# Two moves in TensorE's order and one in the load order of a hybrid decoder step: keys turned later, merge gates cut by contraction tile, one weight block ahead of a cached block

## The chip, the cores and the metric

The kernel runs on one core of one Trainium2 chip. The metric is device time in microseconds (us): the median of three runs. One more execution was taken by the hardware profiler; its span goes from its first instruction to its last.

## What is computed

One inference step of a two-layer decoder, on 256 prompt tokens and 8 sequences of 8 new tokens each (320 columns in all). Each layer runs two token mixers side by side, merges them by gates, and then a gated ConvFFN:

```
hq, hf, hi, hg, nq, kc, vc, ks, vs, kw, vw, ngate, mgate = jnp.split(h @ w_in, splits, axis=-1)
o_hg, s_hg = hgrn2_mixer(...)                     # state recurrence over chunks, one state per head
q = rope_partial(heads(nq, NSA_HEADS), pos)
new_slc = jnp.stack([rope_partial(heads(ks, NSA_KV_HEADS), pos), heads(vs, NSA_KV_HEADS)], axis=2)
kw = rope_partial(heads(kw, NSA_KV_HEADS), pos)
o_win = window_sample(q, pos, kw, vw, past[2])    # samples: window cache and the new rows
o_cmp, o_slc = nsa_cmp_slc(q, pos, cmp_rows, slc_rows, cmp_pe, cmp_w1, cmp_w2)
branches = jnp.einsum('blnc,ncd->blnd', jnp.stack([o_hg, o_nsa], axis=2), w_branch)
mg = jax.nn.sigmoid(mgate.astype(jnp.float32)).reshape(B, L, N_BRANCH, D_MODEL).astype(h.dtype)
merged = jnp.sum(mg * branches, axis=2)
return merged @ w_out, (new_cmp, new_slc, new_win, s_hg)
```

The two parts that matter here are the rotation of queries and keys (`rope_partial`) ahead of the attention scores, and the merge gates (`mgate`): 16 feature tiles per layer, each 128 columns of `w_in` against all 1024 input features.

## The kernel before

Everything is laid out with features on the partitions and the 320 tokens along the free dimension. Each engine has its program written out by hand, layer by layer (`layer(l)` in each block), and the engines meet through semaphores. **TensorE** goes through the layer in this order: input projections, the levels of the HGRN2 recurrence (`level`), the compressor rows (`compressed_rows`), the attention of the prompt in four units (`scores`, `turned`, `values`), the attention of the samples in two halves of four sequences (loop `hb`, from L1179), the HGRN2 outputs, the branch and output projections, the FFN.

PSUM is two rings of four banks, `mm` and `ax`. `mm_plan` and `ax_plan` (L126) list every tile in the order in which it is filled, and name the engine that empties it (V is VectorE, A is ScalarE). A tile may begin when the tile four places ahead of it in its ring has been emptied; `begin` waits for that. ScalarE and VectorE empty tiles in their own programs, in the order of these plans.

Weights and cached rows pass through a ring of four SBUF slots in the order of `BLOCKS` (L67); block n goes to slot n mod 4. SyncE walks `BLOCKS` in its `layer`: at block n it waits until that block's last reader is done (`LAST_USE`), then issues the load of block n + 4 into the slot. So the place of a block in the list sets what its successor's load waits for. `mgN` holds the merge-gate columns of feature tiles 2N and 2N + 1, `kv0` and `kv1` the cached rows of the two halves, `st0` and `st1` the old HGRN2 states of the samples for heads 0, 1 and heads 2, 3 (1 MB each), `br0` and `br1` the branch projection. `LAST_USE` of `mgN` is the gate tile `mgb{2N+1}`, of `kv0` and `kv1` the value products `ov5` and `ov7`.

**Keys.** GpSimd rotates the keys in `stok` in three pieces (L2312 to L2318) and counts `k_roped` (L2319). TensorE transposes them as `kt0` and `kt1` (L1091): six transposes that wait for the third `k_roped`. They stand between `compressed_rows(0)` and `compressed_rows(1)`. Behind `compressed_rows(1)` come the four products `nqr0` to `nqr3`, which permute the queries for their rotation; then `rows_turned(NSEQ)` (tile `cp`), `compressed_rows(2)`, and the compressor's hidden layer. ScalarE empties `kt0` (L1419), VectorE `kt1` (L1939) ahead of `nqr0` to `nqr3`.

**Merge gates in the sample stage.** A gate tile is eight products, one per 128 input features (`feature_tile`). Gates 4 to 7 are made later from split operands. Of gates 0 to 3 the sample stage makes six tiles, three in each half, where other engines are busy with the softmax:

```
GATES = [[(1, 0), (1, 1), (2, 0)], [(2, 1), (3, 0), (3, 1)]]
```

In half `hb` with n = 4 + 2 hb the order is: keys of the cached rows transposed (`skt`), state products (`ds`), `sample_scores(n)`, gate, `sample_scores(n+1)`, `sample_turned(n)`, gate, `sample_values(n)`, `sample_turned(n+1)`, gate, `sample_values(n+1)`. In the first half four of the first gate's eight products stand ahead of `turned(3)` instead. In the second half `sample_rows_turned(1)` (tile `ovt1`) follows, then `prompt_outputs` and `sample_outputs`, which reads `st0` and, from its head 2 on, `st1`.

The helper at L671 records all matmuls, the one at L674 all transposes, so in the rows below those two lines stand for many places.

Of the kernel before, what the change touches and what calls it, by code (L numbers as in the profile page):

```python
# [37 lines left out]
ACT = mybir.ActivationFunctionType  # L38
AX = mybir.AxisListType

P = 128
# [4 lines left out]
KD = D // P  # L46
# [17 lines left out]
DOWN = [[6, 6, 6, 4], [6, 8, 8]]  # L64


BLOCKS = (["par", "w_hf", "w_hq", "w_nq", "cmp", "w_hi", "w_kvn", "w_kvc", "w_cmp", "w_hg", "kv0", "mg0", "mg1", "kv1",  # L67
           "st0", "mg2", "st1", "br0", "mg3", "br1", "wo0", "wo1"] + [f"ff{n}" for n in range(NJ // JPB)]
          + [f"dn{mh}_{n}" for mh in range(2) for n in range(len(DOWN[mh]))])
NBLK = len(BLOCKS)  # L70
# [56 lines left out]
def ax_plan():  # L127
    out = [("cst", "V"), ("norm1", "A"), ("rst", "V")]
    out += level_plan(0) + level_plan(1) + level_plan(2) + [(f"cc{s}", "A") for s in range(4)]
    out += level_plan(3) + level_plan(4) + level_plan(5) + level_plan(6) + [(f"cc{s}", "A") for s in range(4, NSEQ)]  # L130
    out += [("kt0", "A"), ("kt1", "V")] + [(f"nqr{m}", "V") for m in range(4)]
    out += [("cp", "A"), ("hidk", "A"), ("hidv", "A"), ("gsel0", "V"), ("gsel1", "V")]
    out += [("kcm", "A")] + [(f"vc{n}", "A") for n in range(3)] + [("kcr", "V")]
    out += [(f"krt{h}", "AV"[h % 2]) for h in range(HH)] + [("scc0", "V"), ("scc1", "V")]

    def turned(n):
        return [(f"tp{n}_{x}", "AV"[x % 2]) for x in range(2 * (UNITS[n][0] + 1))] + [(f"tpc{n}", "A")]

    def scored(n):
        return [(f"sc{n}_{e}", "V") for e in range(4)]  # L140

    out += scored(0) + scored(1) + turned(0) + scored(2) + [("ov0", "V")] + turned(1) + [("ov1", "V")] + turned(2)
    out += scored(3) + [("ov2", "V")]
    for hb in range(2):
        out += [(f"skt{hb}_{x}", "A" if hb == 0 else "AV"[x % 2]) for x in range(4)] + ([("ovt0", "V")] if hb else [])
        out += turned(3) if hb == 0 else []
        out += [(f"ds{c}", "V") for c in (2 * hb, 2 * hb + 1)] + ([("ov3", "V")] if hb == 0 else [])
        n = 4 + 2 * hb
        out += [(f"ss{x}{n + g}", "A") for g in range(KVH) for x in "ab"]
        out += [(f"tps{n}", "V"), (f"tpn{n}", "A"), (f"ov{n}", "V"), (f"tps{n + 1}", "V"), (f"tpn{n + 1}", "A"),  # L150
                (f"ov{n + 1}", "V")] + ([("ovt1", "V")] if hb else [])
    out += [("op0", "V"), ("op1", "V"), ("os0", "V"), ("os1", "V")]
    for h in range(HH):
        if h == 2:
            out += [(f"xt{x}", "V") for x in range(HH)]
        out += [(f"dsa{h}", "V"), (f"dsb{h}", "V")]
    for n in range(2):
        out += [(f"br{x}{m}", "V") for x in "ba" for m in range(4 * n, 4 * n + 4)]
    out += [("norm2", "A")]
    out += [(f"cv{n}", "V") for n in range(6)]  # L160
    return out + [(f"dn1_{m}", "V") for m in range(4)]
# [73 lines left out]
def hybrid_step(nc, x_prompt, x_sample, cache_cmp, cache_slc, cache_win, state_hgrn, state_conv, page_table, norm_mix,  # L235
# [4 lines left out]
    with ctx:  # L240
# [420 lines left out]
        def _(pe):  # L661
# [50 lines left out]
                              k == KD - 1)  # L712
                last.then_inc(mm_full[L], 1)

            def feature_tile(name, w, cols, half=None):

                bank = MM[L].bank(name) if half == 1 else begin(MM[L], name)
                for k in range(KD) if half is None else range(4 * half, 4 * half + 4):
                    last = mm(bank[:, 0:T], cols(w, k), hT[:, k, :], k == 0, k == KD - 1)
                if half != 0:  # L720
                    last.then_inc(mm_full[L], 1)

            def end_sums(tiles):
# [186 lines left out]
                        last = tr(bank[:, P * x:P * x + P], oX[x][:, h, :])  # L910
                    last.then_inc(ax_full[L], 1)

            def merge_gate(m, y, l, half=None):
                mg = f"mg{m // 2}"
                if m % 2 == 0 and y == 0:
                    pe.wait_ge(*landed_at(mg, l))
                w = kt_of(mg, KD, 512)
                feature_tile(f"mg{'ab'[y]}{m}", w, plain(w, 256 * y + P * (m % 2)), half)

            def level(kk):  # L920
                m = LEVELS[kk]
# [134 lines left out]
            def layer(l):  # L1056
# [31 lines left out]
                for q in range(4, NSEQ):  # L1088
                    rows_turned(q)
                compressed_rows(0, l)  # L1090
                for x in range(2):  # L1091
                    bank = begin(AXR[L], f"kt{x}")
                    if x == 0:
                        pe.wait_ge(k_roped[L], 3)
                    for i in range(3):
                        last = tr(bank[:, P * i:P * i + TM[i]], stok[0:TM[i], i, 256 * x:256 * x + P])
                    last.then_inc(ax_full[L], 1)
                compressed_rows(1, l)
                for m in range(4):
                    bank = begin(AXR[L], f"nqr{m}")  # L1100
                    pe.wait_ge(*MM[L].emptied_at(f"nq{m}"))
                    mm(bank[:, 0:T], con("perm"), qraw[:, m, :], True, True).then_inc(ax_full[L], 1)
                rows_turned(NSEQ)
                compressed_rows(2, l)

# [73 lines left out]
                for hb in range(2):  # L1179
# [6 lines left out]
                            last = tr(bank[:, P * y:P * y + P], kv[:, w, 2 * bp + y // 2, y % 2, 0:P])  # L1186
                        last.then_inc(ax_full[L], 1)
                    if hb == 0:
                        merge_gate(*GATES[0][0], l, 0)
                        turned(3)  # L1190
                    else:
                        sample_rows_turned(0)
# [13 lines left out]
                    pe.wait_ge(*AXR[L].emptied_at(f"skt{hb}_2"))  # L1206
                    n = 4 + 2 * hb
                    sample_scores(n, hb, 0)
                    merge_gate(*GATES[hb][0], l, None if hb else 1)
                    sample_scores(n + 1, hb, 1)  # L1210
                    sample_turned(n)
                    merge_gate(*GATES[hb][1], l)
                    sample_values(n, hb, 0)
                    sample_turned(n + 1)
                    merge_gate(*GATES[hb][2], l)
                    sample_values(n + 1, hb, 1)
                    if hb:
                        sample_rows_turned(1)

                pe.wait_ge(s_ready[L], 3)  # L1220
# [92 lines left out]
        def _(sc):  # L1313
# [38 lines left out]
            def layer(l):  # L1352
# [56 lines left out]
                for i in range(3):  # L1409
# [4 lines left out]
                    else:  # L1414
                        A(gts[0:SMP, i, :], bank[SMP:P, 116:140], ACT.Sigmoid)
                        A(ctok[0:SMP, i, 140:256], bank[SMP:P, 0:116], ACT.Copy)
                        A(ctok[0:SMP, i, 0:140], bank[0:SMP, 0:140], ACT.Copy).then_inc(*st.up(mm_act[L]))
                    if i == 0:
                        bank = take(AXR[L], "kt0")  # L1419
                        A(ktn[:, 0, :], bank[:, 0:T], ACT.Copy).then_inc(*st.up(ax_act[L]))  # L1420
                    if i == 1:
                        sc.wait_ge(*st.settled())
                        pair_rows(NSEQ, ctok[:, 0:2, :])
                        bank = take(AXR[L], "cp")
                        A(cmp_rows(NSEQ), cmp_bank(bank), ACT.Copy).then_inc(*st.up(ax_act[L]))

# [223 lines left out]
        def _(ve):  # L1650
# [63 lines left out]
            def layer(l):  # L1714
# [221 lines left out]

                link(V.tensor_tensor(qL[:, :, :], qH[:, :, :], pH[:, :, :], ALU.mult))
                ve.sem_inc(*st.up(ql_ready[L]))
                bank = take(AXR[L], "kt1")  # L1939
                V.tensor_copy(ktn[:, 1, :], bank[:, 0:T]).then_inc(*st.up(ax_dve[L]))  # L1940
                for m in range(4):
                    bank = take(AXR[L], f"nqr{m}")
                    V.tensor_tensor(qT[:, m, :], bank[:, 0:T], con("sinq"), ALU.mult).then_inc(*st.up(ax_dve[L]))
                for m in range(4):
                    link(V.tensor_tensor(qraw[:, m, :], qraw[:, m, :], con("cosq"), ALU.mult))
                    V.tensor_tensor(qT[:, m, :], qT[:, m, :], qraw[:, m, :], ALU.add).then_inc(*st.up(q_ready[L]))
# [532 lines left out]
```

## Time and profile before

| | |
|---|---|
| three runs | 1179.44, 1179.52, 1180.67 us; median 1179.52 us |
| profiled execution | 1179.78 us, of which the span is 1178.0 us |
| TensorE (PE) busy | 1148.1 us, 97% of the span; mean granted clock 0.99 |
| TensorE weight loads (PEld) | 1036.2 us, 88% |
| VectorE (DVE) / ScalarE (ACT) / GpSimd (POOL) | 706.7 us, 60% / 544.7 us, 46% / 174.1 us, 15% |
| chain of work that ended last | PE 91% |
| HBM traffic | 143 GB/s over the span |

TensorE is busy almost throughout, so a microsecond is won or lost where it waits, or where its granted clock is below full. The lists below come from one execution: a start and a length in us, the engine, the line, output<-input; the bracket at a row's end is the engine's idle time before it and who ended it. Rows of the second layer lie some 571 us behind those of the first.

### The profile page before, as it was taken

Reading aid. Unit: us, or ns where it says so; the run is one execution under the profiler, and the core shown is the slowest. Engines: PE = TensorE matmul, PEld = TensorE weight load, DVE = VectorE, ACT = ScalarE, POOL = GpSimd, SP = SyncE. Lnnn points to the kernel's source line nnn. Section 1 sums busy time; section 2 is a strip of 40 time slices with the busy share of each in tenths; the row PEclk is TensorE's granted clock in tenths of the full one; section 3 lists DMA queues with packets and bytes.
Section 4 is the critical chain, followed back from the end, with each engine's and each line's share of the span. In section 5 each row is a group of like instructions: output and inputs, shape, how many; then the busy total and the mean of one; then the engine's idle time right before and its main releaser. Section 6 shows DMA issues by size and latency. Waiting matters only on the chain.

```text
span 1178.0 us, 21121 instructions
## 1 busy us (share of the span) xinstructions
PE 1148.1 (97%) x8613; PEld 1036.2 (88%) x8613; DVE 706.7 (60%) x1302; ACT 544.7 (46%) x867; POOL 174.1 (15%) x300
## 2 busy tenths in 40 slices
PE   6999999999999999999999999999999999999997
PEld 5987767678999999999999777667899999999997
DVE  5686255457567777763568633644756677777442
ACT  4532256464355555533454223664634555555232
POOL 1154300002120100100114441000311110010000
PEclk9999999999999999999999989999999999999998
DMA  9554422157644444334456525203784445432411
GB/s 289 163 148 164 155 73 72 42 167 209 237 143 144 143 144 145 124 127 158 144 126 208 170 73 177 72 1 110 198 275 148 143 157 160 158 131 90 145 59 45
DMA packets 151498, 165.99 MB, mean 141 GB/s; under 512 B 31492, under 2 KB 114214, under 8 KB 151078
## 3 DMA queue, kind: packets, MB, share of 16 engines
q1 hardware_dynamic: 151402, 164.64, 44.7%
q8 instruction: 68, 1.11, 0.4%
q14 instruction: 28, 0.23, 0.1%
HBM read 156.22 MB, written 12.46 MB: 143 GB/s over the span
## 4 chain that ended last, share of the span: by engine, by line
PE 91%; DVE 3%; POOL 1%; DMA 1%; ACT 1%; issue 1%; SPq 0%; DVEq 0%; POOLq 0%; ACTq 0%
PE mm L671 65%; PE ax L671 23%; PE ax L674 4%; DMA ring<-in_state_conv 1%; ACT mixb L1317 1%; DMA ring<-in_state_hgrn 1%; POOL rtmp L2315 0%; DVE ring_low L1674 0%; POOL rtmp L2312 0%; POOL work L2318 0%; DVE mixb L1824 0%; DVE mixb L2089 0%; ACT attb L1317 0%; POOL work L2317 0%; DVE work_parts L2058 0%
## 5 line engine op out<-in xcount | busy, mean ns | idle before, releaser
L671 PE MATMUL mm<-work_parts 128*128 128x320 f32 (+2 forms) x1120 | 356.4, 318 | 1.1 <-DVE h_low L1668 1.1
L1674 DVE TENSOR_TENSOR ring_low<-ring,work_parts 128x2048 fp32r<-128x2048 f32 (+2 forms) x116 | 256.0, 2207 | 125.4 <-ACT work_parts L1317 124.7
L671 PE MATMUL mm<-h_low,work_parts 128*128 128x320 f32 x1024 | 319.2, 312 | 0.0
L671 PE MATMUL mm<-work_parts,ring_low 128*128 128x320 f32 x1024 | 315.5, 308 | 0.0
L1317 ACT ACTIVATE work_parts<-ring 128x2048 fp32r<-128x2048 f32 (+2 forms) x116 | 211.9, 1826 | 159.6 <-PE mm L671 90.3
L671 PEld LDWEIGHTS mm<-work_parts 128*128 128x128 f32 (+1 forms) x1120 | 209.1, 187 | 9.2 <-issue 2.0
L671 PEld LDWEIGHTS mm<-h_low,work_parts 128*128 128x128 f32 x1024 | 192.9, 188 | 0.3
L671 PEld LDWEIGHTS mm<-work_parts,ring_low 128*128 128x128 f32 x1024 | 193.0, 188 | 0.0
L671 PE MATMUL ax<-act_parts,work_parts 128*128 128x320 f32 x544 | 126.1, 310 | 0.6 <-DVE ring L2080 0.6
L671 PE MATMUL mm<-act_parts,work_parts 128*128 128x320 f32 x480 | 117.4, 310 | 0.3 <-DVE merged_low L2058 0.3
L671 PE MATMUL mm<-hT,ring 128*128 128x320 f32 x384 | 111.9, 445 | 0.0
L671 PEld LDWEIGHTS mm<-hT,ring 128*128 128x128 f32 x384 | 72.6, 194 | 29.8 <-issue 3.4
L671 PEld LDWEIGHTS ax<-act_parts,work_parts 128*128 128x128 f32 x544 | 92.0, 188 | 2.5 <-DVE ring_low L1674 2.2
L671 PE MATMUL mm<-act_parts,ring_low 128*128 128x320 f32 x304 | 93.9, 309 | 0.0
L671 PE MATMUL ax<-act_parts,ring_low 128*128 128x320 f32 x304 | 93.9, 309 | 0.0
L1317 ACT ACTIVATE attb<-attb,prm 128x256 f32<-128x256 f32 x88 | 41.1, 514 | 92.4 <-DVE attb L2178 92.4
L671 PEld LDWEIGHTS mm<-act_parts,work_parts 128*128 128x128 f32 x480 | 82.9, 188 | 0.8 <-DVE merged_low L2058 0.8
L1317 ACT ACTIVATE attb<-ax 128x512 f32<-128x512 f32 (+4 forms) x56 | 34.4, 675 | 49.9 <-PE ax L674 44.0
L671 PEld LDWEIGHTS mm<-act_parts,ring_low 128*128 128x128 f32 x304 | 57.1, 188 | 0.0
L671 PEld LDWEIGHTS ax<-act_parts,ring_low 128*128 128x128 f32 x304 | 57.1, 188 | 0.0
L2345 POOL TENSOR_TENSOR ring<-ring,mixb 128x1024 f32<-128x1024 f32 x8 | 15.2, 1917 | 244.3 <-PE ax L671 244.3
L2184 DVE TENSOR_TENSOR attb<-mm,work 128x320 f32<-128x320 f32 x44 | 21.7, 492 | 49.3 <-PE mm L671 49.3
(235 smaller groups left out, 1593.6 us busy)
## 6 DMA issues: line engine op xcount, KB each, us to landing
ring<-in_w_gate_up SPq DMA_DIRECT2D x44, 1024.0 KB, 6.9
ring<-in_w_in SPq DMA_DIRECT2D x10, 2048.0 KB, 8.3
ring<-in_w_in SPq DMA_DIRECT2D x18, 1024.0 KB, 7.7
ring<-in_w_down SPq DMA_DIRECT2D x8, 1536.0 KB, 6.7
ring<-in_w_out SPq DMA_DIRECT2D x4, 2048.0 KB, 13.8
ring<-in_w_down SPq DMA_DIRECT2D x4, 2048.0 KB, 8.6
ring<-in_w_in SPq DMA_DIRECT2D x32, 128.0 KB, 3.1
ring<-in_cache_cmp_kv SPq DMA_DIRECT2D x32, 128.0 KB
```

The costliest lines, as they stand in the source:

```text
L671: return nc.tensor.matmul(out, lhsT, rhs, start=start, stop=stop)
L674: return nc.tensor.transpose(out, in_, ident[0:in_.shape[0], 0:in_.shape[0]])
L1317: return nc.scalar.activation(out, in_, f, **kw)
L1674: V.tensor_tensor(unit_of(u, ring_r), unit_of(u, ring), unit_high(u).bitcast(F32), ALU.subtract).then_inc(*st.up(w_low[l]))
L2184: V.tensor_tensor(ut, bank[:, 0:T], rs[:, 0:T], ALU.mult).then_inc(*st.up(mm_dve[L]))
L2345: G.tensor_tensor(s0, s0, end.to_broadcast([P, NSEQ, HD]), ALU.mult).then_inc(*st.up(decayed[L]))
```

## The change

Three edits. `merge_gate` takes a range of products instead of a half.

- `kt0` and `kt1` move behind `nqr0` to `nqr3` in TensorE's order, in `ax_plan` and in the orders of ScalarE and VectorE.
- The 24 gate products of each half are cut at other points (`merge_products`): 3, 7, 7, 7 in the first half, 8, 7, 7, 2 in the second, where the last two stand behind `sample_values(7)`. Before they stood 4, 4, 8, 8 and 8, 8, 8.
- `mg0` and `kv0` change places in `BLOCKS`.

```diff
-"w_hg", "kv0", "mg0", "mg1", "kv1",
+"w_hg", "mg0", "kv0", "mg1", "kv1",
...
-    out += [("kt0", "A"), ("kt1", "V")] + [(f"nqr{m}", "V") for m in range(4)]
+    out += [(f"nqr{m}", "V") for m in range(4)] + [("kt0", "A"), ("kt1", "V")]
...
-            def feature_tile(name, w, cols, half=None):
+            def feature_tile(name, w, cols, first=0, end=KD):
-                bank = MM[L].bank(name) if half == 1 else begin(MM[L], name)
-                for k in range(KD) if half is None else range(4 * half, 4 * half + 4):
+                bank = MM[L].bank(name) if first else begin(MM[L], name)
+                for k in range(first, end):
                     last = mm(bank[:, 0:T], cols(w, k), hT[:, k, :], k == 0, k == KD - 1)
-                if half != 0:
+                if end == KD:
                     last.then_inc(mm_full[L], 1)
...
+            def merge_products(hb, at, n, l):
+
+                for g in range(3):
+                    first, end = max(at - KD * g, 0), min(at + n - KD * g, KD)
+                    if first < end:
+                        merge_gate(*GATES[hb][g], l, first, end)
...
                     if hb == 0:
-                        merge_gate(*GATES[0][0], l, 0)
+                        merge_products(0, 0, 3, l)
                         turned(3)
...
                     sample_scores(n, hb, 0)
-                    merge_gate(*GATES[hb][0], l, None if hb else 1)
+                    merge_products(hb, 0 if hb else 3, 8 if hb else 7, l)
                     sample_scores(n + 1, hb, 1)
                     sample_turned(n)
-                    merge_gate(*GATES[hb][1], l)
+                    merge_products(hb, 8 if hb else 10, 7, l)
                     sample_values(n, hb, 0)
                     sample_turned(n + 1)
-                    merge_gate(*GATES[hb][2], l)
+                    merge_products(hb, 15 if hb else 17, 7, l)
                     sample_values(n + 1, hb, 1)
                     if hb:
+                        merge_products(1, 22, 2, l)
                         sample_rows_turned(1)
```

On TensorE, first layer, behind the end of `compressed_rows(0)` (its products with 256 and 24 columns): the rows with `k_roped_0` are `kt0` and `kt1`, the four with 320 columns `nqr0` to `nqr3`. Before:

```order
L671 MATMUL mm<-ring,hT 128x24 x8
L674 MATMUL ax<-consts,work 128x128 [waits k_roped_0,ax_emptied_by_act_0]
...
L671 MATMUL mm<-ring,hT 128x256 [waits mm_emptied_by_act_0]
L671 MATMUL mm<-ring,hT 128x256 x7
L671 MATMUL mm<-ring,hT 128x24 x8
L671 MATMUL ax<-work,consts 128x320 [waits mm_emptied_by_dve_0,ax_emptied_by_act_0] x3
```

Now:

```order
L671 MATMUL mm<-ring,hT 128x256 [waits mm_emptied_by_act_0]
L671 MATMUL mm<-ring,hT 128x256 x7
L671 MATMUL mm<-ring,hT 128x24 x8
L671 MATMUL ax<-work,consts 128x320 [waits mm_emptied_by_dve_0,ax_emptied_by_act_0] x4
L674 MATMUL ax<-consts,work 128x128 [waits k_roped_0,ax_emptied_by_dve_0]
L674 MATMUL ax<-consts,work 128x128
```

The wait for the keys stands behind 16 + 4 products that stood behind it. In the second layer the rows are the same.

On TensorE, at the end of the second half's gates, up to `ovt1` (the transpose out of `attb`) and `prompt_outputs` (out of `mixb`); the first row belongs to `sample_turned(7)`, the 320-column rows are gate products, the rest between them is `sample_values(7)`:

```order
 L674 MATMUL ax<-consts,pcs 15x128
+L671 MATMUL mm<-hT,ring 128x320
 L671 MATMUL mm<-hT,ring 128x320 [waits mm_emptied_by_act_0]
-L671 MATMUL mm<-hT,ring 128x320 x7
+L671 MATMUL mm<-hT,ring 128x320 x5
 L671 MATMUL ax<-work,attb 128x64 [waits ax_emptied_by_act_0,ax_emptied_by_dve_0]
 L671 MATMUL ax<-work,attb 128x64
 L671 MATMUL ax<-work,attb 32x64 x4
 L671 MATMUL ax<-ring,work 32x64 x16
+L671 MATMUL mm<-hT,ring 128x320 x2
 L674 MATMUL ax<-consts,attb 128x128 [waits ax_emptied_by_dve_0]
```

The last product of the last gate, `mgb3`, stands behind `sample_values(7)` now; it stood ahead of it.

On SyncE, first layer, behind the loads of `kv1`: the state rows are `st0`, then `st1`; the `w_in` rows are `mg2`; `w_branch` (`br0`), not shown, follows:

```order
 L481 DMA ring<-in_cache_win_kv 128x512
-L481 DMA ring<-in_state_hgrn 128x8x128 [waits ax_full_0]
+L481 DMA ring<-in_state_hgrn 128x8x128 [waits mm_full_0]
 L481 DMA ring<-in_state_hgrn 128x8x128
-L481 DMA ring<-in_w_in 128x8x256 [waits mm_full_0]
+L481 DMA ring<-in_w_in 128x8x256 [waits ax_full_0]
 L481 DMA ring<-in_w_in 128x8x256
 L481 DMA ring<-in_state_hgrn 128x8x128 [waits mm_full_0]
```

`st0` waits for a gate now (`mgb1`), and `mg2` for `ov5`. `st1` waits for `mgb3` in both versions.

## Rows read from the trace of the kernel before

**Rows 1.** The page: busy us, share of the span, instructions.

```profile
PE 1148.1 (97%) x8613; PEld 1036.2 (88%) x8613; DVE 706.7 (60%) x1302; ACT 544.7 (46%) x867; POOL 174.1 (15%) x300
```

**Rows 2.** Waits of TensorE: us in total, times, longest.

```profile
PE ax L674 <- POOLq L2319: 5.7, 2, 2.8
PE ax L674 <- DVE attb L2034: 2.7, 2, 1.4
...
PE ax L674 <- DVE attb L2044: 0.9, 2, 0.4
...
PE ax L671 <- DMA ring<-in_state_hgrn: 0.6, 1, 0.6
```

**Rows 3.** Timeline, first layer: `compressed_rows(0)`, keys, `compressed_rows(1)`.

```profile
114.18 5.32 PE L671 MATMUL mm<-ring,hT 128*128 128x256 f32 x32
122.34 1.31 PE L674 MATMUL ax<-consts,work 128*128 128x128 f32 x6 [2.85 <-POOLq L2319]
123.59 6.88 PE L671 MATMUL mm<-ring,hT 128*128 128x256 f32 x32
```

**Rows 4.** Timeline, second layer: the keys.

```profile
693.97 1.87 PE L674 MATMUL ax<-consts,work 128*128 128x128 f32 x6 [2.84 <-POOLq L2319]
```

**Rows 5.** Windows: us, busy time of each engine, PEclk, DMA share, GB/s.

```profile
119.50:135.03 15.53, 12.69 (x82) 10.57 (x84) 4.18 (x10) 3.11 (x7) 4.81 (x10) 0.89 0.24 69
...
215.09:223.40 8.31, 8.31 (x67) 5.91 (x68) 3.58 (x18) 5.65 (x16) 0.00 (x0) 0.79 0.00 1
786.20:792.84 6.64, 6.64 (x68) 4.83 (x68) 3.58 (x18) 5.65 (x16) 0.00 (x0) 1.00 0.00 0
```

**Rows 6.** Window of the second layer behind the wait for the keys.

```profile
694.00:700.00 6.00, 6.00 (x16) 4.30 (x17) 0.49 (x1) 0.44 (x1) 2.83 (x1) 0.50 0.37 112
```

**Rows 7.** Timeline, sample stage: first half's first gate piece and wait; second half; one whole gate.

```profile
209.55 2.42 PE L671 MATMUL mm<-hT,ring 128*128 128x320 f32 x8
...
214.68 0.35 DVE L2034 TENSOR_SCALAR attb<-attb,wt 128x256 f32<-128x256 f32 x1
...
215.09 1.36 PE L674 MATMUL ax<-consts,attb 128*128 128x128 f32 x6 [1.35 <-DVE attb L2034]
...
240.77 0.35 DVE L2034 TENSOR_SCALAR attb<-attb,wt 128x256 f32<-128x256 f32 x1
...
241.71 0.87 PE L674 MATMUL ax<-consts,attb 128*128 128x128 f32 x6
...
793.66 4.47 PE L671 MATMUL mm<-hT,ring 128*128 128x320 f32 x16
```

**Rows 8.** Timeline, second layer, `sample_values(7)` to `sample_outputs`; SPq is SyncE's queue.

```profile
823.01 0.90 PE L671 MATMUL ax<-work,attb 64*128 64x64 f32 x12
823.11 0.99 SPq L481 DMA_DIRECT2D ring<-in_state_hgrn  x2
824.56 2.28 SPq L481 DMA_DIRECT2D ring<-in_w_branch  x3
824.93 0.30 PE L674 MATMUL ax<-consts,attb 128*128 128x128 f32 x1 [0.44 <-DVE attb L2044]
828.96 0.65 PE L671 MATMUL ax<-ring,mixb 128*32 128x128 f32 x16
830.23 0.64 PE L671 MATMUL ax<-ring,mixb 128*32 128x128 f32 x16 [0.63 <-DMA ring<-in_state_hgrn]
```

**Rows 9.** Timeline, first layer: loads of `st0` and `st1`, and the head of `sample_outputs`.

```profile
230.17 1.02 SPq L481 DMA_DIRECT2D ring<-in_state_hgrn  x2
...
253.67 0.99 SPq L481 DMA_DIRECT2D ring<-in_state_hgrn  x2
...
259.52 1.08 PE L671 MATMUL ax<-ring,mixb 128*32 128x128 f32 x32
```

**Rows 10.** DMA issues of `st0`, first layer: both, then the first alone; KB, median us to landing.

```profile
ring<-in_state_hgrn SPq DMA_DIRECT2D x2, 512.0 KB, 4.7
...
ring<-in_state_hgrn SPq DMA_DIRECT2D x1, 512.0 KB, 4.0
```

More of the change, by code:

```diff
@@ L64 @@
 DOWN = [[6, 6, 6, 4], [6, 8, 8]]
-BLOCKS = (["par", "w_hf", "w_hq", "w_nq", "cmp", "w_hi", "w_kvn", "w_kvc", "w_cmp", "w_hg", "kv0", "mg0", "mg1", "kv1",
+BLOCKS = (["par", "w_hf", "w_hq", "w_nq", "cmp", "w_hi", "w_kvn", "w_kvc", "w_cmp", "w_hg", "mg0", "kv0", "mg1", "kv1",
            "st0", "mg2", "st1", "br0", "mg3", "br1", "wo0", "wo1"] + [f"ff{n}" for n in range(NJ // JPB)]
@@ L911, in outputs_turned, with merge_gate @@
                     last.then_inc(ax_full[L], 1)
-            def merge_gate(m, y, l, half=None):
+            def merge_gate(m, y, l, first=0, end=KD):
                 mg = f"mg{m // 2}"
-                if m % 2 == 0 and y == 0:
+                if m % 2 == 0 and y == 0 and first == 0:
                     pe.wait_ge(*landed_at(mg, l))
                 w = kt_of(mg, KD, 512)
-                feature_tile(f"mg{'ab'[y]}{m}", w, plain(w, 256 * y + P * (m % 2)), half)
+                feature_tile(f"mg{'ab'[y]}{m}", w, plain(w, 256 * y + P * (m % 2)), first, end)
+            def merge_products(hb, at, n, l):
[3 more added lines that the diff above has]
+                        merge_gate(*GATES[hb][g], l, first, end)
             def level(kk):
@@ L1090, in layer @@
                 compressed_rows(0, l)
+                compressed_rows(1, l)
+                for m in range(4):
+                    bank = begin(AXR[L], f"nqr{m}")
+                    pe.wait_ge(*MM[L].emptied_at(f"nq{m}"))
+                    mm(bank[:, 0:T], con("perm"), qraw[:, m, :], True, True).then_inc(ax_full[L], 1)
                 for x in range(2):
@@ L1097, in layer @@
                     last.then_inc(ax_full[L], 1)
[L1098 to L1102, printed above, removed]
                 rows_turned(NSEQ)
@@ L1423, in layer @@
                         pair_rows(NSEQ, ctok[:, 0:2, :])
+                        bank = take(AXR[L], "kt0")
+                        A(ktn[:, 0, :], bank[:, 0:T], ACT.Copy).then_inc(*st.up(ax_act[L]))
                         bank = take(AXR[L], "cp")
@@ L1943, in layer @@
                     V.tensor_tensor(qT[:, m, :], bank[:, 0:T], con("sinq"), ALU.mult).then_inc(*st.up(ax_dve[L]))
+                bank = take(AXR[L], "kt1")
+                V.tensor_copy(ktn[:, 1, :], bank[:, 0:T]).then_inc(*st.up(ax_dve[L]))
                 for m in range(4):
```

5 lines of the change are left out of this document (removed).

## The prediction

> **What bounds the kernel now.** Read the page first: TensorE is busy 1148.1 of 1178.0 us [rows 1]. The busy sum of the matmuls does not tell where the time could come from, so the second view is the list of TensorE's own waits. One stands out, and it comes once per layer: transposes that wait for GpSimd's line 2319, 5.7 us in two. That line is the count of rotated keys, so these are `kt0`. Next come 2.7 us in two for VectorE's line 2034, the scaled probabilities of the samples, and 0.9 us in two for line 2044 [rows 2]. The third view is the timeline around each wait, and the fourth the granted clock there, since a wait can cost more than its length. In the first layer `compressed_rows(0)` takes 5.32 us; its twin `compressed_rows(1)`, the same products, takes 6.88 us right behind the wait [rows 3]. The windows say why: from 119.5 to 135.03 the mean granted clock is 0.89, and in the second layer six us behind the wait run at 0.50, the 1.2 GHz level [rows 5, 6]. So the price of a wait is its idle time and, sometimes, some microseconds at half clock behind it.
>
> The sum is made against the profiled execution, 1179.8 us (span 1178.0 and 1.8 around it), which lies 0.3 us above the median of the runs. A change below 0.2%, 2.4 us, would pass for no change; faster means below 1177.1, slower above 1181.9.
>
> **Keys behind the queries.** TensorE ends `compressed_rows(0)` at 114.18 + 5.32 = 119.5 and could transpose keys only at 122.34 [rows 3]. Now `compressed_rows(1)` comes first: 5.32 us at full clock, to 124.8, 2.5 us behind the keys, with `nqr0` to `nqr3` still to come. In the second layer the wait begins at 693.97 - 2.84 = 691.13 [rows 4]; 5.32 us more is 696.4, again 2.5 us behind. Both waits go: 2.85 + 2.84 = 5.7 us. With them goes the half clock: 0.11 of the 15.53 us in the first layer is 1.7 us, and half of the 6.0 us in the second is 3.0 us [rows 5, 6]. The moved instructions are the same six transposes, one ScalarE and one VectorE copy per layer, at no new cost. What is new is that `kt0` waits for VectorE to have emptied `nqr0`, which it does while TensorE still makes `nqr2` and `nqr3`, and that ScalarE copies `kt0` between the new compressor rows and `cp`; TensorE has `compressed_rows(2)` to do meanwhile. I take nothing for that; if the cover failed, the bounds are nothing and the length of the wait it replaces. **Gain 10.4 us.**
>
> **Gate pieces, first half.** The wait for line 2034 stands at `sample_turned(4)`. The scores end at 209.55, the scaled probabilities at 214.68 + 0.35 = 215.03, a chain of 5.5 us on VectorE and ScalarE. TensorE had four gate products and the next scores to do, until 215.09 - 1.35 = 213.74 [rows 7]. Now it has seven products. One product is 4.47 / 8 = 0.56 us [rows 7], three are 1.7 us, more than the 1.35 us, with 0.3 us to spare. Both waits go, 2.7 us. Behind it the first layer's clock fell and the second's did not: the same work takes 8.31 us at 0.79 and 6.64 us at 1.00 [rows 5], so 1.7 us more go. **Gain 4.4 us.** The pieces elsewhere get one product thinner. In the second half the piece ahead of `sample_turned(6)` keeps its eight, and there the margin is 241.71 - 241.12 = 0.6 us [rows 7]. No other wait shows in these places; between nothing and 0.56 us in each I take 0.2 us in all.
>
> **Two products ahead of `ovt1`.** The transpose at 824.93 waited 0.44 us for line 2044, in both layers [rows 2, 8]. Two products, 1.1 us, now cover that. **Gain 0.9 us.**
>
> **`st1` comes later.** This is the step that costs. `st1` goes into the slot of `mg1`, and SyncE loads it when `mgb3` is done. In the second layer that was at 823.01; the load went out at 823.11, and TensorE needed head 2 at 828.96 + 0.65 = 829.6 and got it at 830.23, so it paid 0.63 us [rows 8]. The budget was 6.6 us, the landing took 7.1 us from the first issue. Now the last two products of `mgb3` stand behind `sample_values(7)`. What lay between them and `ovt1`, 823.01 to 824.93, is lost from the budget: 6.6 - 1.9 = 4.7 us. How fast will `st1` land? The upper row is the 7.1 us. The lower is `st0`, the same size and also followed by another load one microsecond behind: 4.0 us for its first issue, 4.7 in the median of both, so 5.4 us for the second, which goes out half a microsecond later, 5.9 us in all [rows 9, 10]. In the first layer `st1` left at 253.67 and was there by 260.1, when head 2 ran without a gap: at most 6.4 us [rows 9]. So the wait is 1.3 to 2.5 us per layer. I take 1.6 us in the first layer, nearest to its own row, and 1.9 us in the second, of which 0.6 us is paid today: **cost 2.9 us**, bounds 2.0 and 4.4 us.
>
> Then the clock behind it. Idle times of 2.85 us were followed by a half clock in both layers, 1.35 us in one of two, 0.63 us not. For a wait of 1.3 to 2.5 us I take one fall in the two layers, at the mean of the three falls above, (1.7 + 3.0 + 1.7) / 3: **cost 2.1 us**, bounds nothing and 6.0 us.
>
> [...]
>
> **`mg0` ahead of `kv0`.** `mg0` is loaded earlier than it was. `kv0` goes out behind `compressed_rows(2)`, done by 135.03 [rows 5], and is first read at the head of the sample stage, a few us ahead of 209.55 [rows 7]; the store issues queued behind it and the load of `mg1` move back by its issues, with tens of microseconds in hand. `st0` now waits for `mgb1` instead of `ov5` and goes out earlier. None of these was waited for, so I take nothing.
>
> **Sum.** Gains 10.4 + 4.4 + 0.9 = 15.7 us; costs 2.9 + 2.1 + 0.2 = 5.2 us; net 10.5 us: 1179.8 - 10.5 = **1169.3 us**.
>
> **The rivals.**
>
> *The state load is in time.* If both halves of `st1` landed as the first half of `st0` did, in 4.0 us, the load would be there 4.6 us after `mgb3`, inside the budget; the 0.6 us paid today would go too: 1179.8 - 15.7 - 0.6 + 0.2 = 1163.7 us. Against it: 5.9 and 7.1 us for the same megabyte, and a second half that always queues behind the first. "DMA: Bandwidth & Descriptors" of the Trainium skill, section "Specifications", gives about 0.6 us to the first byte and 358 GB/s, which makes an estimate of 3.5 us; no run here shows that. Chance 7%.
>
> *The sample stage gets its waits back.* The 0.3 us to spare is thin; ScalarE and VectorE meet the gates at other points, and any wait there may bring the low clock with it. If nothing is won in that half, the 4.4 us go: 1173.7 us. Chance 10%.
>
> *The change doesn't do what it says.* If what ended the wait was not the keys alone, `kt0` would wait at its new place about as long, for banks or for its copies, and the 10.4 us would stay lost: 1179.7 us, no change. Against it: GpSimd's line 2319 is named in both layers. Chance 4%.
>
> *Slower: the state wait keeps the clock down.* At `sample_outputs` TensorE would sit idle 1.3 to 2.5 us behind many small products, and if the granted clock then stayed at 0.50 through the split gates and branch products, half of that stretch would be lost. It decides from 12.6 + 2.4 = 15 us lost, that is 15 us at half clock in each layer. The falls seen cost 1.7 to 3.0 us each. With 20 us low per layer: 1179.8 - 12.6 + 20 = 1187.2 us. Chance 3%.
>
> **How the numbers follow.** The forecast's own case holds 76%: 1167.2 without a fall of the clock, 1169.3 with one, 1171.4 with two. With the state load at its lower bound 1166.3; with its upper bound and two falls of 3.0 us 1174.7. The second rival lies inside. So the range is 1166.0 to 1174.5 us; outside are the first, third and fourth rival, 14%, and the tails. Faster: 76 + 7 + 10 = 93%; same 4%; slower 3%.
>
> **What would show it.** Right: no wait for GpSimd's line 2319 in TensorE's list, and the two `compressed_rows` of a layer equally long, near 5.3 us; no wait for line 2034; a wait for `in_state_hgrn` in both layers, 1.3 to 2.5 us each, with `st1` issued a quarter microsecond ahead of `ovt1`; perhaps a window at half clock behind it. Wrong: `kt0` idle at its new place; new waits between gate pieces; no wait for the states, or one above 3 us; or a mean granted clock below today's 0.99.

## The result and the profile after

Six runs of the changed kernel: 1166.02 to 1174.71 us, median **1168.62 us**; the kernel before beside it 1180.28 us. The ratio of the changed kernel to the one before is 0.9908, with a 95% interval of [0.9883, 0.9934]; ratios here are worked out from all runs of both kernels and are not quite the quotient of the medians. Run twice more, the changed kernel gave 0.9907 [0.9884, 0.9931] and 0.9928 [0.9907, 0.9948]; the median of its 18 runs is 1169.5 us. The forecast was 1169.3 us, range 1166.0 to 1174.5. One run of `e1_keys_only` (5256.74 us) and one of `e3_swap_only` (4196.26 us) lie far above all others; they count in no ratio below, and the medians of these two are of their other runs.

The profiled execution took 1166.02 us, span 1164.2, mean granted clock 0.996. The page's busy line, beside [rows 1], and TensorE's waits, beside [rows 2]:

```profile
PE 1142.0 (98%) x8613; PEld 1032.4 (89%) x8613; DVE 707.1 (61%) x1302; ACT 544.1 (47%) x867; POOL 173.2 (15%) x300
```

```profile
PE ax L674 <- DMA attb<-in_norm_final: 8.0, 1, 8.0
PE ax L671 <- DMA ring<-in_state_hgrn: 2.7, 2, 1.4
PE mm L671 <- DVE h_low L1675: 1.1, 1, 1.1
PE ax L671 <- DVE attb L1855: 0.9, 2, 0.5
PE ax L671 <- DVE ring L2087: 0.6, 2, 0.3
PE ax L671 <- ACT mixb L1325: 0.6, 2, 0.3
```

The first row is the wait for the first load at the kernel's start. It heads the list of before too, with 8.3 us, ahead of the rows in [rows 2]:

```profile
PE ax L674 <- DMA attb<-in_norm_final: 8.3, 1, 8.3
```

The waits for the keys (5.7 us), for the scaled probabilities (2.7) and ahead of `ovt1` (0.9) are gone; the wait for the old states has grown from 0.6 to 2.7 us. The rest, from 1.1 us down, are small and belong to work that the change leaves alone. The timeline of the first layer shows each place. The 64 products are `compressed_rows(0)` and `(1)` without a gap, 10.57 us for both where the two of [rows 3] took 5.32 and 6.88 with 2.85 us between them; then the queries and, last, the six key transposes:

```profile
113.86 10.57 PE L671 MATMUL mm<-ring,hT 128*128 128x256 f32 x64
124.27 2.40 PE L671 MATMUL ax<-work,consts 128*128 128x320 f32 x8
126.51 1.16 PE L674 MATMUL ax<-consts,work 128*128 128x128 f32 x6
```

In the sample stage the six transposes of the scaled probabilities carry no bracket either, where [rows 7] has 1.35 us. At the end of the second half come the two products that were put there (two instructions each, as in the 16 of a whole gate in [rows 7]), `ovt1` without a gap, and then `sample_outputs` with its wait for `st1`:

```profile
206.47 1.83 PE L671 MATMUL ax<-work 64*32 64x256 f32 x28
208.24 0.87 PE L674 MATMUL ax<-consts,attb 128*128 128x128 f32 x6
...
244.30 1.34 PE L671 MATMUL mm<-hT,ring 128*128 128x320 f32 x4
245.48 0.27 PE L674 MATMUL ax<-consts,attb 128*128 128x128 f32 x1
...
249.47 0.64 PE L671 MATMUL ax<-ring,mixb 128*32 128x128 f32 x16
251.42 0.64 PE L671 MATMUL ax<-ring,mixb 128*32 128x128 f32 x16 [1.31 <-DMA ring<-in_state_hgrn]
```

SyncE's queue, beside [rows 9]: `st0` leaves 17.7 us earlier than before, of which some 7 us are the lead that the whole kernel has by then (the six transposes start at 208.24, before at 215.09). `st1` leaves at 245.68, and TensorE could go on 5.7 us later.

```profile
212.48 1.26 SPq L481 DMA_DIRECT2D ring<-in_state_hgrn  x2
...
245.68 0.99 SPq L481 DMA_DIRECT2D ring<-in_state_hgrn  x2
246.72 2.59 SPq L481 DMA_DIRECT2D ring<-in_w_branch  x3
```

**Where the rest came from: the granted clock.** The idle time won is 5.7 + 2.7 + 0.9 - 2.1 = 7.2 us, but the profiled times differ by 13.8. The other 6.6 us lie in stretches below full clock while TensorE worked; the windows below are laid around all of them, in both kernels. Columns: window and length, busy time of PE, PEld, DVE, ACT and POOL, PEclk, DMA share, GB/s. Before:

```profile
120.00:132.00 12.00, 9.65 (x44) 7.92 (x45) 1.32 (x3) 1.54 (x5) 4.50 (x9) 0.86 0.29 82
153.00:165.00 12.00, 11.61 (x88) 8.62 (x87) 7.15 (x42) 5.70 (x22) 0.00 (x0) 0.86 0.55 176
210.00:222.00 12.00, 10.65 (x60) 6.91 (x58) 6.47 (x35) 9.00 (x27) 0.00 (x0) 0.86 0.00 1
690.00:702.00 12.00, 9.16 (x40) 7.24 (x39) 0.49 (x1) 0.90 (x3) 5.68 (x13) 0.72 0.43 119
```

The changed kernel has one such window, in the last part of the second layer:

```profile
1143.00:1158.00 15.00, 13.39 (x94) 12.80 (x92) 3.32 (x9) 2.98 (x9) 0.00 (x0) 0.86 0.00 1
```

The length times (1 - PEclk) is the time lost: before 1.7 + 1.7 + 1.7 + 3.4 = 8.4 us (from unrounded terms), after 15 x 0.14 = 2.1 us. TensorE's last product ends at 1156.6, and 0.4 of the 2.1 us lie behind it; up to there 1.7 us are lost. So 7.2 + 6.7 = 13.9 us stand against the 13.8. The first, third and fourth window of before stand behind the waits for the keys and for the scaled probabilities, as the prediction had it. The second does not: the clock fell right behind 48 small matmul instructions with 15 output columns (at 157.3), with 0.3 us of idle time ahead of them. Nor does the window of after: the clock fell at the end of 24 instructions with a single output column (at 1146.9), ahead of the last split products, and no wait is there. The first two rows are of before, the other two of after:

```profile
152.16 1.47 PE L674 MATMUL ax<-consts,mixb 128*128 128x128 f32 x12
153.94 3.30 PE L671 MATMUL ax<-work 64*128 64x15 f32 x48 [0.31 <-ACT mixb L1317]
...
1142.61 1.47 PE L674 MATMUL mm<-consts,hT 128*128 128x128 f32 x12
1143.91 3.02 PE L671 MATMUL ax<-consts,mixb 128*128 128x1 f32 x24
```

The one-column work ran at full clock in the profile of before. Twelve transposes stand just ahead of both places; whether they or the narrow products matter for the fall was not separated.

So the question for the experiments: does the clock's share belong to the edits, as the prediction booked it, or does it come and go?

### The profile page after: what moved, and what is told of

It reads as the page before. It is cut to its first block, busy times and chain, and to the rows that moved or that the text cites. A ratio compares the mean times of both kernels' runs of the same rounds, so it can differ in the third digit from the quotient of the medians.

```text
span 1164.2 us, 21121 instructions
## 1 busy us (share of the span) xinstructions
PE 1142.0 (98%) x8613; PEld 1032.4 (89%) x8613; DVE 707.1 (61%) x1302; ACT 544.1 (47%) x867; POOL 173.2 (15%) x300
## 4 chain that ended last, share of the span: by engine, by line
PE 94%; DVE 2%; DMA 1%; ACT 1%; issue 0%; SPq 0%; DVEq 0%; ACTq 0%
PE mm L671 66%; PE ax L671 23%; PE ax L674 5%; DMA ring<-in_state_hgrn 1%; ACT mixb L1325 1%; DMA attb<-in_norm_final 0%; DVE ring_low L1681 0%; DVE mixb L1831 0%; DVE mixb L2096 0%; DVE work_parts L2065 0%; PE mm L674 0%; DVE mixb L1848 0%; DVE mixb L2097 0%; DVE merged_low L2065 0%; DVE mixb L2250 0%
## 6 DMA issues: line engine op xcount, KB each, us to landing
ring<-in_w_out SPq DMA_DIRECT2D x4, 2048.0 KB, 13.9
```

## The experiments

### One part of the change at a time

`e1_keys_only` is the kernel before with the keys moved behind the queries on all three engines and in `ax_plan`; `e2_gates_only` has only the new cuts of the gates; `e3_swap_only` only the swap in `BLOCKS`.

```diff
 e1
-    out += [("kt0", "A"), ("kt1", "V")] + [(f"nqr{m}", "V") for m in range(4)]
+    out += [(f"nqr{m}", "V") for m in range(4)] + [("kt0", "A"), ("kt1", "V")]
 e2
-                        merge_gate(*GATES[0][0], l, 0)
+                        merge_products(0, 0, 3, l)
...
+                        merge_products(1, 22, 2, l)
 e3
-"w_hg", "kv0", "mg0", "mg1", "kv1",
+"w_hg", "mg0", "kv0", "mg1", "kv1",
```

> The kernel before with only the keys moved behind the rotated queries. Theory (a wait costs its idle time and the half clock that often follows): both waits for GpSimd's line 2319 go, 5.7 us, and the falls behind them, 4.7 us; ratio 0.991, some 1170 us; the waits for the scaled probabilities (2.7 us) stay. Rival (the clock falls as often wherever TensorE next idles a little, whatever is removed): only the idle time goes, 5.7 us, ratio 0.995.

Measured: 1173.50 us against 1179.68, so 6.2 us by the medians; ratio 0.9941 [0.9928, 0.9955], that is 7.0 us, 5.3 to 8.5. The theory's 10.4 us lies outside, the rival's 5.7 inside: this is the idle time and little of the clock. TensorE's waits and the low windows of its profile (1174.06 us):

```profile
PE ax L674 <- DVE attb L2033: 2.7, 2, 1.4
...
PE ax L671 <- DMA ring<-in_state_hgrn: 0.8, 1, 0.8
```

```profile
204.00:216.00 12.00, 10.65 (x60) 7.02 (x58) 6.62 (x35) 8.99 (x27) 0.00 (x0) 0.86 0.00 1
...
714.00:726.00 12.00, 11.62 (x89) 8.74 (x87) 7.25 (x42) 5.66 (x22) 0.00 (x0) 0.86 0.55 176
771.00:783.00 12.00, 10.65 (x62) 7.17 (x60) 6.33 (x35) 9.32 (x28) 0.00 (x0) 0.86 0.00 1
...
1149.00:1164.00 15.00, 14.75 (x95) 14.35 (x93) 2.65 (x7) 1.41 (x3) 0.00 (x0) 0.77 0.00 1
```

Behind the keys there is no low window any more. But the scaled probabilities now have one in both layers, where before had it in one; the 15-column products have one in the other layer; and the one-column products at the end have one. Together 3 x 1.7 + 3.4 = 8.5 us, as much as before. In this execution the low clock was not saved, it stood elsewhere; its five runs have clocks of 0.987 to 0.993, with 0.992 in the middle, and the kernel before beside them 0.990.

> The kernel before with only the gate products cut at the new points. Theory: the waits for the scaled probabilities (2.7 us) and ahead of ovt1 (0.9 us) go, waits for the states of 1.3 to 1.4 us per layer come in place of 0.6 us: idle time 1.5 us less in all; with the clock's falls undecided the ratio is 0.996 to 1.002. Rival (the state load still lands in time when mg0 and kv0 are not exchanged): 3.6 us and a fall less, ratio 0.995.

Measured: 1181.09 us, ratio 1.0011 [0.9997, 1.0026]; the granted clocks of its 12 runs are 0.981 to 0.991, those of the kernel before beside it 0.988 to 0.991. The theory's range was 0.996 to 1.002. Its waits (profiled 1185.87 us), and two of its low windows:

```profile
PE ax L674 <- POOLq L2327: 5.6, 2, 2.8
PE ax L671 <- DMA ring<-in_state_hgrn: 3.0, 2, 1.8
```

```profile
825.00:837.00 12.00, 10.21 (x156) 7.87 (x153) 8.33 (x8) 6.82 (x10) 2.73 (x2) 0.72 0.94 256
1161.00:1176.00 15.00, 15.00 (x80) 14.67 (x80) 1.86 (x5) 0.94 (x2) 0.00 (x0) 0.61 0.00 0
```

The waits for the scaled probabilities and ahead of `ovt1` are gone as in the changed kernel, the state wait is there, in sum 1.3 us less idle time. But one of the state waits was followed by a low stretch (825 to 837, 3.4 us lost) and the end of the kernel had another (5.9 us), while those behind the keys stayed. Alone this edit is worth nothing. That is no blow to the prediction's sum: its own terms for the gates, 4.4 + 0.9 - 0.2 of gains and 2.9 + 2.1 of costs, leave 0.1 us. But they reach it by less low clock in the sample stage, and the profile shows more low clock in all.

> The kernel before with only mg0 and kv0 exchanged in the load order. Theory: nothing on TensorE waited for these loads, so no wait changes and the ratio is 1.000 within 0.2%. Rival (the earlier load of the first two states takes load off the queue ahead of the second two): the 0.6 us wait for the states goes, still within 0.2%; a new wait for the cached rows would show at the head of the sample stage and cost up to some us.

Measured: 1179.97 us, ratio 1.0001 [0.9992, 1.001]. The swap alone does nothing. The three ratios multiply to 0.9953, with an interval of about 0.993 to 0.998 worked out from the three; the change has 0.9908, 0.9907 and 0.9928, and the last is the one taken on the same chip as the three parts. To see whether the swap makes the difference beside the others, it was undone in the changed kernel:

```diff
-"w_hg", "mg0", "kv0", "mg1", "kv1",
+"w_hg", "kv0", "mg0", "mg1", "kv1",
```

> The changed kernel with the first cached block ahead of the first merge block again, as before the change. My theory: the swap is worth nothing by itself or beside the rest, so the ratio to the kernel before lies where the changed kernel lies on this chip (0.9907, from 0.988 to 0.993), with 2.7 to 2.9 us of waiting for the old states and no wait for the keys or the scaled probabilities. Then what the two other parts give together and not apart (keys only 0.9941, gates only 1.0011, product 0.9952) is between these two alone. Rival: the missing 5 us come from the swap beside the others; then the ratio is near 0.995 and a wait for the first merge block or the first cached block shows on TensorE.

Measured: 1171.73 us, ratio 0.9925 [0.9904, 0.9946], beside 0.9928 for the changed kernel on the same chip, with a state wait of 2.8 us in two and no new one. So the swap is worth nothing beside the others either, and what is more than additive lies between the keys and the gates. How much that is stays unsure: on this chip 3 us, with intervals that overlap, and some 5 us by the two other ratios.

### Is the clock's share fixed? The changed kernel again

> The changed kernel again, beside the others on this chip. Theory: median 1168 to 1170 us, spread of some 8 us between runs, with the mean granted clock between 0.99 and 0.996 in step with the time: a hundredth of clock is some 12 us. Rival (the spread is waits that differ from run to run): times that do not follow the clock.

> The changed kernel once more, beside these two: 0.9907 as twice before, spread over 8 to 9 us, with a granted clock from 0.990 to 0.997, and the long executions those with the low clock. In its profile the long and the short differ in where TensorE is at half clock: one stretch at the end alone, or one behind the second state's wait as well.

Measured: 1168.09 us (1164.69 to 1173.34) and 1170.93 us (1166.01 to 1174.24). The times follow the clock: of the 18 runs the four at 0.996 and 0.997 took 1164.7 to 1168.2 us, the five at 0.988 to 0.990 took 1171.9 to 1174.7. The waits of the three profiles are the same within 0.2 us, the low windows are not. Of the second profile (1170.01 us) and of the third (1169.36 us):

```profile
816.00:828.00 12.00, 12.00 (x139) 10.00 (x132) 8.36 (x10) 5.64 (x9) 3.79 (x2) 0.57 0.65 163
1143.00:1158.00 15.00, 15.00 (x115) 14.81 (x114) 2.36 (x6) 1.41 (x3) 0.00 (x0) 1.00 0.01 1
```

```profile
813.00:825.00 12.00, 10.54 (x172) 9.25 (x171) 10.66 (x11) 8.54 (x11) 3.79 (x2) 1.00 0.89 231
1143.00:1158.00 15.00, 15.00 (x86) 14.72 (x83) 2.00 (x6) 0.94 (x2) 0.00 (x0) 0.66 0.01 1
```

In the second the clock fell behind the state wait of the second layer (12 x 0.43 = 5.2 us) and not at the end; in the third at the end (5.1 us) and not behind the same wait. One program, the same waits, 1.7 to 5.2 us of low clock in one place or another.

### The state load

`e4_tail_before_values` puts the last two products of the second half back ahead of `sample_values(7)`, so that `mgb3` ends and `st1` is asked for earlier. `e5_ovt1_inside` does the same and makes `ovt1` inside `prompt_outputs`, behind its first eight products. `e6_states_second` keeps the changed kernel's gates and lets `sample_outputs` do heads 0 and 1 wholly, for both of its tiles, before it waits for `st1`. `e7_states_behind_branch` makes the wait longer: SyncE asks for `st1` behind the three loads of `br0`.

```diff
 e4, e5
-                    merge_products(hb, 15 if hb else 17, 7, l)
+                    merge_products(hb, 15 if hb else 17, 9 if hb else 7, l)
...
-                        merge_products(1, 22, 2, l)
 e5
-                        sample_rows_turned(1)
...
 e5, in prompt_outputs
                     inner_part(banks[1], 3, h)
+                sample_rows_turned(1)
 e6, in sample_outputs
+                banks = [begin(AXR[L], f"os{y}") for y in range(2)]
+                for part in range(2):
+                    pe.wait_ge(*landed_at(f"st{part}", l))
...
+                    for y in range(2):
...
 e7, SyncE
+                        if b == "mg1":
+                            continue
                         load(BLOCKS[(n + NSLOT) % NBLK], lay + (n + NSLOT) // NBLK)
+                        if b == "kv1":
+                            load("st1", lay)
```

> The changed kernel with the last two gate products of the second half back ahead of its last value products (8, 7, 9). Theory (the late last product is what makes the states late): the waits for the states fall from 2.7 us in all to at most 0.7 us, the wait ahead of ovt1 comes back with 0.4 us per layer; 1.2 us less idle time than the changed kernel, some 1166 to 1167 us median, and, if these waits bring its clock falls, a narrower spread than 1166.0 to 1174.7. Rival (the states are late for another reason, the load order): the waits for the states stay at 2.7 us and the time rises by 0.9 us.

Measured: 1167.16 us, ratio 0.9887 [0.9873, 0.9901]. The trade shows as it was priced:

```profile
PE ax L674 <- DVE attb L2050: 0.9, 2, 0.4
...
PE ax L671 <- DMA ring<-in_state_hgrn: 0.4, 1, 0.4
```

The 0.9 us ahead of `ovt1` come back and 2.3 us of state wait go, so in idle time the two products behind `sample_values(7)` cost 1.4 us more than they win.

> The changed kernel with the last two gate products ahead of the last value products (8, 7, 9) and ovt1 set behind the first eight products of the prompt outputs. Theory: neither the states nor ovt1 are waited for, or the states by some 0.3 us at most; 2.1 to 2.7 us less idle time than the changed kernel, 1165 to 1166 us if its median stays at 1168.6, less where falls of the clock behind the state waits go too. Rival (ScalarE's copy behind ovt1 is what ends the stage): a new wait ahead of the split gates of up to 1 us per layer.

Measured: 1167.58 us, ratio 0.9899 [0.9884, 0.9913]; no wait ahead of `ovt1`, 1.1 us for the states in one layer. A new gap of 0.6 us stands ahead of the split gates in the first layer, as the rival had it, though in one layer only and with no releaser that the profile shows:

```profile
PE mm L671 <- issue: 0.6, 1, 0.6
```

> The changed kernel with the sample outputs in another order: heads 0 and 1 of both halves first, heads 2 and 3 (st1) behind them, 1.5 us later than now. Theory: the waits of 1.3 to 1.4 us per layer for the states go to nothing, 2.7 us less idle time than the changed kernel, and fewer falls of the clock. Rival (the lower clock comes from elsewhere): 2.7 us less, the same spread between runs.

Measured: 1167.36 us, ratio 0.9902 [0.9888, 0.9915]; no wait for the states. The changed kernel beside e5 to e7 had 0.9907, and its own spread of 8.7 us covers differences of this size: neither e5 nor e6 is shown to be faster than it. Nor is e4, whose interval overlaps those of the changed kernel's first two ratios.

> The changed kernel with the load of st1 issued behind the three loads of br0 (2 MB). Theory (the wait for the states has a price per microsecond, and a longer idle time brings the clock down): st1 goes out 2.6 us later and behind 2 MB more, so the wait grows from 1.3 to 7 to 10 us per layer; with a fall of the clock behind each, 1.7 to 3 us: 15 to 23 us more than the changed kernel. Rival (loads share the queues and st1 lands about as fast from its issue): 2.6 us more per layer, 5 to 8 us in all.

Measured: 1194.99 us, ratio 1.0124 [1.0103, 1.0145], 27 us above the changed kernel on that chip, more than the 15 to 23 expected. Its wait, and the windows behind it (profiled 1195.80 us); TensorE resumed at 262.0 and 838.8:

```profile
PE ax L675 <- DMA ring<-in_state_hgrn: 19.3, 2, 10.1
```

```profile
261.00:270.00 9.00, 8.01 (x122) 5.54 (x123) 1.37 (x2) 1.20 (x3) 1.31 (x1) 0.59 0.15 39
270.00:273.00 3.00, 3.00 (x22) 3.00 (x21) 2.42 (x5) 2.95 (x4) 2.49 (x2) 1.00 0.03 5
...
838.00:849.00 11.00, 10.19 (x127) 7.73 (x127) 2.97 (x5) 3.35 (x5) 3.49 (x2) 0.51 0.07 20
849.00:855.00 6.00, 6.00 (x40) 5.38 (x40) 3.09 (x3) 2.72 (x5) 0.30 (x1) 1.00 0.01 3
```

The waits are about as long as expected, 16.4 us more idle time than in the changed kernel beside it. The clock fell in both layers while TensorE waited, 9 x 0.41 = 3.7 and 11 x 0.49 = 5.4 us by these windows; the first 1.0 and 0.8 us of them are still idle, so at most 0.5 and 0.4 of that cost nothing. So the falls cost 3.2 to 3.7 and 5.0 to 5.4 us, where 1.7 to 3 each were expected. The clock was back within 8 and about 10 us of the restart, through the same small products and split gates. Even behind 9 and 10 us of idle time it does not stay down.

### Both repairs together

`e9_inside_and_states_second` is e5 and e6 in one kernel.

> The changed kernel with both repairs: the last turned rows of the samples are made inside the prompt's outputs, so that the second state is asked for about 1.5 us earlier, and the outputs of the samples take heads 0 and 1 wholly before they wait for it. No wait of TensorE for the states or for the turned rows should be left, idle time 2.7 us under that of the changed kernel's profile. Theory (a wait of 1.3 to 1.6 us costs its own length and, in a part of the executions, a stretch at half clock behind it): the median falls by 1 to 3 us under the changed kernel on the same chip, to a ratio of 0.988 to 0.990, and the spread is under 6 us. Rival: half-clock stretches only go elsewhere, to places with as little work in them; then the median is within 1 us of the changed kernel and the spread is as wide (9 us).

Measured: **1165.48 us**, ratio 0.9879 [0.9859, 0.9898], beside 0.9928 [0.9907, 0.9948] for the changed kernel on the same chip. The intervals do not touch: beside each other this version beats both kernels, though the changed kernel's two earlier ratios, 0.9908 and 0.9907, have intervals that reach into its own. No wait for the states or ahead of `ovt1` is left. It gains more than the 2.9 us of idle time, 5.4 us by the medians; its five runs also had the higher clocks (median 0.995 against 0.992), which by the rest of this section may be chance. At 0.990 its two runs took 1169.4 and 1169.7 us, the changed kernel's three at 0.990 took 1171.9 to 1174.7. Its spread is not narrower: 1162.98 to 1169.68 us. The profiled one (1169.41 us) is a long one, low at the 15-column products and at the end:

```profile
711.00:723.00 12.00, 11.69 (x91) 9.12 (x90) 7.51 (x43) 5.95 (x22) 0.00 (x0) 0.86 0.67 210
1143.00:1161.00 18.00, 17.41 (x96) 16.61 (x94) 3.07 (x8) 2.55 (x8) 0.00 (x0) 0.63 0.00 1
```

Up to TensorE's last product at 1160.4 the second stretch costs 6.4 us. So theory and rival both hold a part: the idle time goes for good, the low clock finds other places.

### The account of the profiles

Idle change is the sum of the differences in the four waits of [rows 2]; the other waits are left out, and the one at the kernel's start differs by up to 0.4 us between profiles. Low clock is the sum over the windows, up to TensorE's last product and without the idle part of e7's; the account is 1179.78 us, plus the idle change, plus the low clock less 8.4. The first row's four windows, the single windows of the changed kernel, and those of e1 and e9 stand above; of e2 the account also takes 1.7, 1.7, 3.4 and 1.7 us from four windows at the keys and the 15-column products, both layers. The windows of e3 to e6 and e8, and e7's other three, are not shown.

| profile | idle change | low clock | account | measured |
|---|---|---|---|---|
| before | 0 | 8.4 | | 1179.78 |
| after | -7.2 | 1.7 | 1165.9 | 1166.02 |
| after again | -7.0 | 5.2 | 1169.6 | 1170.01 |
| after, third | -7.0 | 5.1 | 1169.5 | 1169.36 |
| keys only (e1) | -5.5 | 8.5 | 1174.4 | 1174.06 |
| gates only (e2) | -1.3 | 17.9 | 1188.0 | 1185.87 |
| swap only (e3) | 0.5 | 8.4 | 1180.3 | 1179.47 |
| e4 | -8.6 | 8.1 | 1170.9 | 1169.38 |
| e5 | -8.8 | 3.3 | 1165.9 | 1167.42 |
| e6 | -9.9 | 5.1 | 1166.6 | 1167.36 |
| e7 | 9.4 | 14.8 | 1195.6 | 1195.80 |
| without swap (e8) | -7.1 | 6.8 | 1171.1 | 1171.34 |
| both repairs (e9) | -9.9 | 8.1 | 1169.6 | 1169.41 |

Seven of the twelve close within 0.4 us; those of e3 and e6 are 0.8 us off, of e4 and e5 1.5, and the row of the gates 2.1. Of e5's gap 0.6 us are its new wait ahead of the split gates, which is none of the four. In e2 and e4 the account is too long, and both have a low stretch that costs some 6 us and runs to TensorE's last products, where other work may decide the end; but so has e9, which closes. What the rest is was not tried.

## Why the prediction was right, and where it was not

**Keys: idle 5.7 us: right.** Both waits are gone in every kernel with this edit, and `kt0` waits for nothing at its new place. Alone the edit gives 6.2 us by the medians, 7.0 by the ratio.

**Keys: half clock 4.7 us: wrong as a term.** The stretches behind the keys are gone, but the gain is not the keys' own. The step that failed is "With them goes the half clock": in e1's profile the loss was 8.5 us as before, in other places. By the runs the edit's clock share alone is 6.2 - 5.7 = 0.5 us, or 7.0 - 5.7 = 1.3 us by the ratio (2.8 at the end of its interval).

**Gates: idle 2.7 and 0.9 us: right;** the seven products cover the scaled probabilities and the two cover `ovt1` in every kernel that has them. **The 1.7 us of half clock behind it: wrong in the same way;** e2 shows the windows of the sample stage gone and others in their place.

**State wait: right in kind, a little too dear.** The term was 1.6 + 1.9 us less the 0.6 paid before, 2.9 us. The three profiles wait 2.7, 2.9 and 2.9 us, 1.3 to 1.6 in a layer, so the cost is 2.1 to 2.3 us, near the lower bound of 2.0. The mis-sized part is the landing: 5.7 to 6.0 us in the six layers, where the prediction went by 5.9 to 7.1. The budget was a little shorter too: `st1` left 0.2 us behind the start of `ovt1` and not a quarter of a microsecond ahead of it, and head 2 was due at 249.47 + 0.64 = 250.11, 4.4 us later and not 4.7. The estimate from the Trainium skill ("DMA: Bandwidth & Descriptors", "Specifications"), 3.5 us for the megabyte, was short of it; the measurement decides.

**One fall behind the state wait, 2.1 us: chance and size were both off, and their product came out near.** The prediction took one fall in two layers, at 2.1 us. In the changed kernel's three profiles the clock fell behind one of six state waits, a third of that chance, and cost 5.2 us there: 1.7 us an execution. The Trainium skill, in "TensorE: Matmul & The Clock Gate", "Loop structure matters more than you think", says that behind a long wait for a DMA, of 8 us in its example, matmuls run at the lower clock. The 9 and 10 us of e7 agree, in both layers; waits of 1.2 to 1.8 us brought the fall in two of ten.

**The swap, 0: right,** alone and beside the rest.

**Not in the prediction:** the low clock at the 15-column products and at the end of the kernel, where no wait is longer than 0.3 us. The first was in the trace of before, but the prediction reads the clock only behind waits; the second was not in that execution at all.

The time came out right by some luck, because two errors met. The prediction took 4.7 + 1.7 - 2.1 = 4.3 us off for the clock; the three profiles have 8.4 less 1.7, 5.2 and 5.1, that is 4.4 us in the mean. It left out 1.7 us of low clock that before also had, at the 15-column products, and it had 2.1 us in the changed kernel where these three have 4.0 in the mean. That the sum agrees does not make its terms right: e1 would have been forecast at 1169.4 us and measured 1173.5.

**The rivals.** The state load in time: no, the wait is in all profiles. The sample stage's waits back: no. The change doing nothing: no. The clock staying down: no; e7 put 9 to 10 us of idle time in the same place, and it was back within 10 us.

**What stays open** is why the keys and the gates together lower the mean loss (granted clock 0.993 in the middle of 18 runs, 0.990 before) when the keys alone did so by a microsecond or so and the gates alone raised it. There are fewer waits left at which the clock can fall, which fits; that it is the cause was not tested by itself. Nor was it tried what decides, in one execution, at which place it falls.

## What to carry to other kernels

Book idle time and low clock apart: the change's idle time could be summed from wait rows to within a microsecond here (6.2 us forecast with its small costs, 7.0 to 7.2 measured). A half-clock stretch seen behind a wait of 1 to 2 us in one execution was a draw, and even where it came behind every wait, as at the keys, as much low clock stood elsewhere in the profile taken without that wait. Look for low-clock windows over the whole span and not only behind waits, and profile a kernel two or three times before the clock's share is credited to an edit. When small edits are judged, compare runs at the same granted clock as well as medians.

## What the hardware showed beyond that

- In or right behind waits of 2.8 us the clock fell each time: six of six, in the profiles of before, e2 and e3. In or behind 1.3 to 1.4 us for the scaled probabilities it fell in four of six layers (before, e1, e3), behind 1.2 to 1.8 us for the states in two of ten (the changed kernel three times, e2, e8).
- It also fell with no wait longer than 0.3 us in front: at or right behind the 48 instructions with 15 output columns in 11 of 26 layers (thirteen profiles), and at or right behind the one-column ones near the end in 10 of 13 profiles, though not in that of before.
- One low stretch cost from 1.7 to 6.4 us (the last in e9). The 18 runs of one unchanged program spread over 10 us in 1169, 0.9%, in step with their clocks, and that is several times what the edits of the state load are worth in idle time. The Trainium skill says, in "TensorE: Matmul & The Clock Gate", "Part 1: The HAM clock gate", that the same kernel shows a different number of slow matmuls from run to run, and speaks there of a kernel's start; the three profiles of the changed kernel agree, for falls in its middle and at its end.
